# A short convolution by Strassen-Winograd products: partial sums formed in the accumulators, weight sums kept in DRAM after the first pass

## The reference, cut to what matters

```python
def _short_conv_mixer(xn, prev, w_in, conv_w, w_out):
    proj = xn @ w_in                       # 1024 -> 4 x 1024
    b_gate, c_gate, h, z = jnp.split(proj, 4, axis=-1)
    u = c_gate * h
    ...
    y = jax.nn.silu(z) * b_gate * conv     # conv: 3 taps over u
    return y @ w_out, up[:, T:]
```

## Time and profile before

| | us |
|---|---|
| median of 3 runs (lowest, highest) | 2836.79 (2834.07, 2838.17) |
| the profiled execution: its time | 2833.93 |
| its span, first to last instruction | 2832.2 |
| first matmul of the first product | 21.4 |
| last matmul of the phase's last product | 808.1 |
| PE busy over the whole span | 2690.6 |

### The profile page before, as it was taken

One profiled execution on the slowest core, in us unless ns is written; L12 is line 12 of the kernel. 1 busy time (PEld: TensorE's weight loads), 2 busy tenths in 40 slices (PEclk: granted clock), 3 DMA queues, 4 the chain that ended last, 5 costly groups with the idle time before them and its releaser, 6 DMA issues. The chain is left out here.

```text
span 2832.2 us, 44315 instructions
## 1 busy us (share of the span) xinstructions
PE 2690.6 (95%) x15048; PEld 2407.0 (85%) x15048; DVE 1998.5 (71%) x2590; ACT 1606.5 (57%) x3224; POOL 1435.6 (51%) x1251
## 2 busy tenths in 40 slices
PE   5997999799899999999989999999999999989998
PEld 5997999799888888889978988888888888877886
DVE  6777766877754460102248999999999999998775
ACT  5564454444333441111147888888888888875543
POOL 5767655776540021003346777777786768652110
PEclk8998999899999999999999999999999999999999
DMA  3332232133244443434578777767676866757873
GB/s 107 118 99 69 85 110 83 51 113 94 71 146 133 131 147 136 178 114 154 164 218 251 216 230 228 207 216 232 196 242 204 244 208 196 234 180 214 245 227 108
DMA packets 371536, 467.40 MB, mean 165 GB/s; under 512 B 53346, under 2 KB 312546, under 8 KB 365316
## 3 DMA queue, kind: packets, MB, share of 16 engines
q1 hardware_dynamic: 364612, 440.69, 51.4%
q0 software_dynamic: 6720, 24.13, 2.6%
HBM read 340.95 MB, written 123.81 MB: 164 GB/s over the span
## 5 line engine op out<-in xcount | busy, mean ns | idle before, releaser
L2318 POOL TENSOR_TENSOR a_a<-a_a,a_prod 128x512 f32<-128x512 f32 (+3 forms) x640 | 662.0, 1052 | 274.1 <-DVE a_prod L2269 196.9
L474 PE MATMUL c_pc<-c_xh,c_wh 128*128 128x384 f32 (+1 forms) x1344 | 453.3, 337 | 58.3 <-DVE c_sums L706 32.8
L2269 DVE TENSOR_TENSOR_SCAN a_prod<-a_keep,a_prod,a_restart 128x513 f32<-128x513 f32 x384 | 478.4, 1270 | 7.6 <-ACT a_keep L2213 7.0
L476 PE MATMUL c_pc<-c_xh,c_wl 128*128 128x384 f32 (+1 forms) x1344 | 449.2, 334 | 0.0
L475 PE MATMUL c_pc<-c_xl,c_wh 128*128 128x384 f32 (+1 forms) x1344 | 449.2, 334 | 0.0
L2212 ACT ACTIVATE a_a<-a_pz 128x512 f32<-128x512 f32 (+3 forms) x640 | 357.4, 559 | 70.2 <-PE a_pz L2139 48.5
L2279 DVE TENSOR_TENSOR a_atl<-a_pt,a_ath 128x512 fp32r<-128x512 f32 (+3 forms) x640 | 363.4, 600 | 31.9 <-ACT a_ath L2222 28.9
L2222 ACT ACTIVATE a_ath<-a_pt 128x512 fp32r<-128x512 f32 (+3 forms) x640 | 332.9, 559 | 56.9 <-PE a_po L2153 33.3
L2213 ACT ACTIVATE a_keep<-a_pz 128x512 f32<-128x512 f32 (+3 forms) x640 | 361.2, 565 | 0.0
L474 PEld LDWEIGHTS c_pc<-c_xh,c_wh 128*128 128x128 f32 x1344 | 261.5, 195 | 63.9 <-DVE c_sums L706 35.9
L2162 PEld LDWEIGHTS a_pt<-ident_r,a_bits 128*128 128x128 f32 x2176 | 231.0, 141 | 52.1 <-DVE a_atl L2279 8.4
(11 more groups left out here) (252 smaller groups left out, 5999.6 us busy)
## 6 DMA issues: line engine op xcount, KB each, us to landing
a_x<-x_d SPq DMA_DIRECT2D x84, 896.0 KB, 7.0
c_raw<-in_a_w_in SPq DMA_DIRECT2D x96, 512.0 KB, 4.1
a_x<-x_d SPq DMA_DIRECT2D x56, 832.0 KB, 5.6
a_kh<-kh_t SPq DMA_DIRECT2D x32, 512.0 KB, 7.1
a_kl<-kl_t SPq DMA_DIRECT2D x32, 512.0 KB, 9.1
x<-f_xn POOLq DMA_DIRECT2D x17, 512.0 KB, 5.2
g_y_in<-sz_t SPq DMA_DIRECT2D x17, 512.0 KB, 8.3
g_x<-x SPq DMA_DIRECT2D x17, 512.0 KB, 4.5
```

The costliest lines, as they stand in the source:

```text
L474: pe.matmul(o, room.wh[i][:, k, :], x_h, start=fresh and k == 0, stop=False, skip_group_check=True)
L476: mm = pe.matmul(o, room.wl[i][:, k, :], x_h, start=False, stop=k == NH - 1, skip_group_check=True)
L2269: dve.tensor_tensor_scan(prod[:, s, 0:w + 1][:, ::-1], keep[:, n % KS, 0:w + 1][:, ::-1], restart[:, 0:1].broadcast_to([P, w + 1]), prod[: ...
L2318: pool.tensor_tensor(part, part, prod[:, n % PS, after:after + w], ALU.mult).then_inc(weighted, 1)
```

## The change

**Passes** are (0, 384), (768, 384), (1536, 320), so six tiles are staged first and eleven later. **Accumulators:** S2_T2 is no longer the first product of bank C: ScalarE copies P1 from bank A into bank C (`move_p1`, PSUM to PSUM) and S2_T2, S3_T3 and A22_T4 add to it, so `v` and c21's sum with P1 are not formed. ScalarE copies S1_T1 (`read_p5`) and u2 (`read_u2`) to SBUF. Two small groups of matmuls at the start write bank C of both sets once. **Combining:** c21 is multiplied straight from PSUM by VectorE into `u` or `t`; GpSimd keeps `set_late_u`, two `gate` and `finish_late` for each pair. `sums` has a tile for each strip of a pair. **Weights:** GpSimd forms S1 to S4 in pass 0 alone, SP stores them to a DRAM tensor (`store_sum`, 256 KB each) and loads them in the passes after (`load_sum`); the raw A21 is then not loaded. `summed` is one semaphore for each sum. **Differences** are all VectorE's (`difference`), S1's and S3's one and two strips before the pass ends. **Tiles:** VectorE scales the first three; A11_B11 and A12_B21 of strip 0 need these alone. `turn` stands between A12_B21 and S4_B22, and ScalarE's `scale` behind `high(n, A22_T4)`. The three taps are loaded from GpSimd's queue.

```diff
-PASSES = [(0, 320), (640, 384), (1408, 384)]
+PASSES = [(0, 384), (768, 384), (1536, 320)]
...
         def _(sp):
...
+            for n in range(NSTRIP):
+                if n + 1 in norm_of:
+                    load_tile(norm_of[n + 1])
+                store_sum(n + 1, 2)
+                load_sum(n + 1, 2)
+                load_sum(n + 2, 0)
+                if n + 2 < NSTRIP:
+                    free_raw(n, 1)
                     load_raw(n + 2, 1)
                 if n >= 2 and n % 2 == 0:
                     store(n - 1)
+                load_sum(n + 2, 1)
                 if n + 3 < NSTRIP:
+                    free_raw(n + 1, 0)
                     load_raw(n + 3, 0)
+                load_sum(n + 2, 3)
+                for k in (0, 1, 3):
+                    store_sum(n + 2, k)
...
         def _(pe):
...
+            for n in range(1, NSTRIP):
                 product(n, A11_B11)
                 product(n, S1_T1)
+                product(n - 1, A22_T4)
                 product(n, S2_T2)
                 product(n, A12_B21)
+                if n - 1 in norm_of:
+                    turn(norm_of[n - 1])
                 product(n, S4_B22)
                 product(n, S3_T3)
...
         def _(act):
...
             for n in range(NSTRIP):
+                if n:
+                    move_p1(n)
                 high(n + 1, A11_B11)
+                if n and n % 2 == 0:
                     open_gate(n - 1)
+                if n % 2 == 0:
                     prefix(n)
+                if n:
+                    read_p5(n)
                 high(n + 1, S1_T1)
                 high(n, A22_T4)
+                if n - 1 in norm_of:
+                    scale(norm_of[n - 1])
+                if n % 2:
                     keep_and_tap(n)
+                if n:
+                    read_u2(n)
                 high(n + 1, S2_T2)
+                read_c11(n)
                 high(n + 1, A12_B21)
+                if n in norm_of:
+                    sums_of(norm_of[n])
                 high(n + 1, S4_B22)
                 high(n + 1, S3_T3)
...
         def _(dve):
...
             for n in range(NSTRIP):
+                p, turning = n // PER_PASS, n % PER_PASS == PER_PASS - 1 and n != LAST
+                if n and not first_of_pass(n):
                     c22(n - 1)
+                low(n, S3_T3)
                 low(n + 1, A11_B11)
+                if turning:
+                    difference(p + 1, S2_T2)
+                if n - 1 in norm_of:
+                    inverse(norm_of[n - 1])
                 low(n + 1, S1_T1)
                 if n:
                     c21(n - 1)
+                if first_of_pass(n):
+                    difference(p, A22_T4)
                 low(n, A22_T4)
                 if n % 2:
                     taps(n)
+                if p < NPASS - 1 and n % PER_PASS in (PER_PASS - 3, PER_PASS - 2):
+                    difference(p + 1, S1_T1 if n % PER_PASS == PER_PASS - 3 else S3_T3)
+                low(n + 1, S2_T2)
+                if turning:
+                    c22(n)
                 low(n + 1, A12_B21)
+                c12(n)
+                low(n + 1, S4_B22)
                 if n - 1 in norm_of:
+                    stage(norm_of[n - 1])
...
         def _(pool):
...
+            for k in (0, 1, 3, 2):
+                sum_weights(0, k)
+            for k in (0, 1, 3):
+                sum_weights(1, k)
             for n in range(NSTRIP + 1):
+                if n % 2:
+                    set_late_u(n - 1)
+                elif n:
                     gate(n - 1, 1)
+                    finish_late(n - 1)
+                sum_weights(n + 1, 2)
+                if n % 2:
+                    gate(n, 0)
+                for k in (0, 1, 3):
+                    sum_weights(n + 2, k)
```

More of the change, by code:

```diff
@@ L227 @@
 NPROD = 7
+SUMS = (S1_T1, S2_T2, S3_T3, S4_B22)
+EARLY_TILES = 3
 BANK_A, BANK_B, BANK_C = range(3)
@@ L265, in __init__ @@
         self.taps = put("c_taps", [P, KT, CW], F32, offset=room_at + 12288)
-        self.s = [put(f"c_s{i}", [P, NH, P], F32, offset=border.at + part * i) for i in range(4)]
+        self.s = [put(f"c_s{i}", [P, NH, P], F32, offset=border.at + part * i) for i in range(len(SUMS))]
         self.put, self.at = put, room_at + 28768
@@ L451, in product @@
                 p = STRIPS[n][0]
-                w, fresh = width(n), i in (A11_B11, S1_T1, S2_T2)
+                w, fresh = width(n), i in (A11_B11, S1_T1)
                 b = {A11_B11: BANK_A, A12_B21: BANK_A, S1_T1: BANK_B, S4_B22: BANK_B}.get(i, BANK_C)
@@ L611, in _ @@
             act.wait_ge(warm, 1)
-            for t in range(FIRST_TILES):
+            for t in range(EARLY_TILES + 1):
                 sums_of(t)
-                if t:
-                    scale(t - 1)
-                if t == 3:
-                    high_w(0, A11_B11)
-                elif t == 4:
-                    high_x(0, A11_B11)
-            scale(FIRST_TILES - 1)
-            high_w(0, S1_T1)
-            high_x(0, S1_T1)
-            for i in (S2_T2, A12_B21, S4_B22, S3_T3):
-                high(0, i)
@@ L625, in _ @@
[L625 to L630 removed]
+            scale(EARLY_TILES)
+            sums_of(EARLY_TILES + 1)
+            high(0, A11_B11)
+            scale(EARLY_TILES + 1)
+            high(0, A12_B21)
+            sums_of(EARLY_TILES + 2)
@@ L631, in _ @@
+            scale(EARLY_TILES + 2)
+            move_p1(0)
+            high(0, S1_T1)
+            high(0, S4_B22)
+            read_p5(0)
+            high(0, S2_T2)
+            high(0, S3_T3)
+            read_u2(0)
+            for n in range(NSTRIP):
+                if n:
+                    move_p1(n)
                 high(n + 1, A11_B11)
-                if m == 0 and n:
+                if n and n % 2 == 0:
                     open_gate(n - 1)
-                if m == 0:
+                if n % 2 == 0:
@@ L648, in _ @@
                 high(n + 1, A12_B21)
+                if n in norm_of:
+                    sums_of(norm_of[n])
                 high(n + 1, S4_B22)
                 high(n + 1, S3_T3)
-                if n in norm_of:
-                    sums_of(norm_of[n])
-                if n - 1 in norm_of:
-                    scale(norm_of[n - 1])
                 if n == LAST:
                     act.wait_ge(border.y_loaded, 16)
-                    for i in (S1_T1, S2_T2, S3_T3, S4_B22):
+                    for i in SUMS:
@@ L687, in stage, with difference @@
                                       gain[:, half].unsqueeze(2).broadcast_to([P, NH, P]), ALU.mult).then_inc(staged, 1)
+            def difference(p, i):
+                first, second, out, needs = {
+                    S1_T1: (room.quarter(p, 0, 1), room.quarter(p, 0, 0), room.operand(p, S1_T1), None),
+                    S3_T3: (room.quarter(p, 1, 1), room.quarter(p, 0, 1), room.quarter(p, 0, 1), S1_T1),
+                    S2_T2: (room.quarter(p, 1, 1), room.operand(p, S1_T1), room.quarter(p, 0, 0), S1_T1),
+                    A22_T4: (room.quarter(p, 1, 0), room.quarter(p, 0, 0), room.quarter(p, 1, 0), S2_T2)}[i]
+                order = (S1_T1, S3_T3, S2_T2, A22_T4)
+                dve.wait_ge(staged, tiles_staged(p))
+                if needs is not None:
+                    dve.wait_ge(t_set[order.index(needs)], p + 1)
+                if i == S2_T2:
+                    dve.wait_ge(x_lo[A11_B11], p + 1)
+                elif i == A22_T4:
+                    dve.wait_ge(x_lo[A12_B21], p + 1)
+                elif i == S1_T1:
+                    wait_past(dve, x_lo[S1_T1], p)
+                dve.tensor_tensor(out, first, second, ALU.subtract).then_inc(t_set[order.index(i)], 1)
             def low_x(p, i):
@@ L702, in low @@
                     low_x(STRIPS[n][0], i)
-            def add(out, n, b, other, read):
-                w = width(n)
-                dve.tensor_tensor(out, bank(n, b, w), other, ALU.add).then_inc(read, 1)
             def c22(n):
@@ L809, in _, with sum_weights @@
         def _(pool):
-            def sums(n):
+            def sum_weights(n, k):
+                if n >= PER_PASS:
+                    return
                 raw = room.raw[n % 2]
                 a11, a12, a21, a22 = raw[:, 0, 0:NH, :], raw[:, 0, NH:KT, :], raw[:, 1, 0:NH, :], raw[:, 1, NH:KT, :]
-                s1, s2, s3, s4 = (s[:, :, :] for s in room.s)
+                s = [tile[:, :, :] for tile in room.s]
+                first, second, op = ((a21, a22, ALU.add), (s[0], a11, ALU.subtract), (a11, a21, ALU.subtract),
+                                     (a12, s[1], ALU.subtract))[k]
@@ L2929, in build @@
     x1 = scratch("x1", [T, D])
+    sums_d = scratch("sums_d", [PER_PASS, len(SUMS), P, NH * P])
     x_d = scratch("x_d", [NGX, P, KT, 2, PW])
```

378 lines of the change are left out of this document (180 added, 198 removed).

## The result

| us | before | after |
|---|---|---|
| median (lowest, highest), 4 runs each on one chip | 2835.43 (2834.04, 2838.17) | 2759.28 (2757.80, 2760.17) |
| the profiled execution: its time, its span | 2833.93, 2832.2 | 2760.17, 2758.5 |
| first matmul of strip 0, of strip 1 | 21.4, 54.7 | 22.9, 56.6 |
| last matmul of the phase's last product | 808.1 | 729.8 |

The ratio is 0.973 (95% interval 0.9713 to 0.9747): 76 us faster, where 2758 was forecast. The phase is 78.3 us shorter by the profiles and the span 73.7. The code behind the phase is the same; over the fourteen profiles of this study it took 2023 to 2030 us, so the 4.6 between the two is no effect of the change.

A forecast was written before the change was run, and what follows sets the result against it. PE was taken as the bound, with 121 us above its pace in the phase. Gains of 30.1 + 29.6 + 14.5 + 3.0 + 1.0 = 78.2 us off 2833.9 gave 2755.7, forecast as 2758, range 2742 to 2786.

The forecast's parts named there:

- The turns: Token-tile transposes in passes 0 and 1: twelve PE waits of 1.92 us, slow clock and one turn go, 30.1 us won.
- The changes of pass: Strips around both pass changes: without GpSimd's weight sums stretching VectorE's subtractions, 29.6 us won, bounds 18 to 34.
- the uncontended walk: Step through strips 15 and 16 with VectorE at its undisturbed times: about 4.4 us lost at a change of pass.
- the contended 9.7: The same walk through strips 15 and 16 with VectorE contended: 9.7 us lost at a change of pass.
- The 7 and 6 that were to stay: Loss still expected after the change: 7 us at the first change of pass, 6 at the narrower second.
- The last pass: From 570 to 808.6 us: waits on c_sums behind GpSimd's late u go, 14.5 us won, bounds 8 to 15.5.
- The start: Up to strip 1: overhead falls from 44.1 to 41.1 us, 3.0 won, bounds 0 to 7; VectorE carries the chain.
- The steady state: Ordinary strips: ScalarE's added copies and the changed VectorE and GpSimd work were all to be hidden.
- the transfers: Loads and stores of weights and sums: DMA share about 0.6, each sum with some 13 us between issue and use.
- 7 us to spare: Pass 0 loop from raw load through three sums to u: sums end 2 to 3 us into the next strip, u due at 7.
- The rival that was to make it slower than before: Sum loads and stores on one queue hold each other up in all passes: 2878 at 5 us a pair; chance 0.04.
- The end: End of the phase: GpSimd's last `finish` falls out ahead of the last store, 1 us won.

The follow-up runs named there:

- u ahead: Kernel before, with GpSimd's second half of u put behind the first of the next strip's four weight sums instead of behind all four: 2871.37 us, ratio 1.0124.
- the third sum late: Kernel before, with GpSimd forming the next strip's sum S3 at the end of its strip, after the gates or second half of u: 2824.65 us, ratio 0.9967.
- the next weights late: Kernel before, with the roundings of the next phase's first five weight slabs all in the last strip, not one a strip from 39: 2831.86 us, ratio 0.9984.
- three copies a strip: Changed kernel, with three unread 512 KB DRAM-to-DRAM weight copies each strip ahead of the second raw load on SP's queue: 2820.3 us, ratio 0.9943.

## Why the prediction was right, step by step

**The turns: right, 30.1 forecast.** No wait of PE on `c_norm` is left from strip 2 on, and a turn costs 0.72, the own time that was put at 0.7. Won are 29.7, with 0.8 lost in strip 1. The slow clock that was counted in went with the idle time: the granted clock is 1.00 in 330 to 530 where it was 0.97. But the term is a place in the ledger, not the worth of the edit. Alone the edit brings 10 us (2833.29 to 2823.05), because in narrow strips `c_sums` takes the place of `c_norm`. The sum was right since the whole change takes that second wait away too, in pass 0 by the width and in the last pass by the new scheme; the prediction had no step for it, and that it came out is in part luck.

**The changes of pass: right, 29.6 forecast, 30.9 measured.** The releaser is the one named, `read_u2` behind the high part of T4, and the first change keeps 6.2, between the 4.4 of the uncontended walk and the contended 9.7. The 7 and 6 that were to stay are 6.2 and 6.0. One low granted stretch of 3.4 us remains in each (windows 280 to 330 and 530 to 575 at 0.97 and 0.96). VectorE's two stretched operations in strip 16 end 0.5 and 1.6 us after GpSimd's. The prediction read the earlier trace rows as an end together with GpSimd's instruction; it too is 0.5 later (247.6 after 247.1), most of the operation's own 0.68. The Trainium skill (SBUF — State Buffer, Who interferes with whom) has one engine held there for the whole of the other's instruction; the trace agrees, 2.56 us for an operation that takes 1.75. By its rule with GpSimd idle the change would have kept 4.4; GpSimd was not idle: the stretch beside its `gate` and `finish`, 1.6 us, is in size nearly the 1.8 between.

**The last pass: right in size (14.5 and 15.3) and in the chain, without the cause ahead of it.** "The chain there: ScalarE's keep_and_tap waits 4.54 us for GpSimd's u, since `set_u` stands behind the sums of the next strip" is what the rows of strips 43 and 44 show, with taps, c22 and PE behind it. But u behind the sums is in every pair; what makes it late in strips 40 to 45 are the next phase's roundings ahead of c22, which the prediction did not name: without them 13 us of stall go. Of the 15.7, moving u ahead wins 2.8 and moving S3 behind u 6.8. The changed kernel keeps the roundings in the same strips and loses 0.4 there, since GpSimd forms no sums; with them (sums in every pass) 5.4 us come back in just these strips. The edits to the kernel before were run one by one, none of them together.

**The start: 3.0 forecast, nothing won.** The 44.1 of overhead stay 44.1. This lies on the lower bound of 0 to 7, and may lie below it. Three of the kernels made from the one before (u ahead, the third sum late, the next weights late) have its code up to strip 1 but for the place of a sum, and reach strip 1 at 52.8, 53.3 and 52.9, where its own profile has 54.7; four with the changed kernel's start reach it at 56.4 to 57.7, beside its 56.6. 1.9 us of the difference are more work (12.5 for 10.6), so against the usual 52.9 the start has become some 2 us slower; the profile of before had a long one. The kernel before with the turn alone agrees, at 52.6. Three parts of the walk were too short. VectorE's reciprocal stands for tile 3, whose square waits for its transfer, and `stage` 1 and 2 stand behind it; the low parts and differences run beside GpSimd's sums and are stretched (the one at 20.07 ends at 22.88, 1.6 us after GpSimd's sum of 19.77 to 21.28); and PE at half clock makes what waits for its products late. Timeline of the changed kernel, the rows for each:

```profile
15.31 0.16 DVE L739 RECIPROCAL c_rstd<-c_std 128x1 f32<-128x1 f32 x1 [2.60 <-ACT c_std L568]
...
20.07 2.81 DVE L778 TENSOR_TENSOR c_xl<-c_stage,c_xh 128x1536 fp32r<-128x1536 f32 x1
...
44.29 2.54 POOL L924 TENSOR_TENSOR c_s<-c_raw,c_s 128x512 f32<-128x512 f32 x1 [0.22 <-issue]
...
45.61 2.84 DVE L773 TENSOR_TENSOR c_stage<-c_stage 128x1536 f32<-128x1536 f32 x1
...
40.80 0.49 ACT L611 ACTIVATE c_p<-c_pc 128x384 f32<-128x384 f32 x1 [4.54 <-PE c_pc L507]
```

The first was tested (the start in another order) and is worth 3.2 us at the first product and about 1 behind strip 2. The other two are read from rows, not tested. VectorE's own scaling was no part of it: 0.75 us where 1.1 was taken.

**The steady state, the transfers, the end.** All of what was called hidden is hidden: no wait in 330 to 530, and 0.4 us in 60 to 280. The third copy of ScalarE, into PSUM, takes 0.47. The DMA share is 0.53 and 0.49, forecast about 0.6, and the stores of the sums land in 2.2 us at the median (60 to 280). "I find 7 us to spare" in the loop of pass 0 was wrong, though it cost nothing: in strip 9, which starts at 176.94, the third sum ends 4.4 us in where 2 to 3 were told, and u at 182.8, 1.2 us ahead of `keep_and_tap`. GpSimd and ScalarE in the timeline of the changed kernel:

```profile
180.06 1.29 POOL L924 TENSOR_TENSOR c_s<-c_raw,c_s 128x512 f32<-128x512 f32 x1 [0.22 <-issue]
181.31 1.46 POOL L939 TENSOR_TENSOR c_u<-c_sums,c_cg 128x384 f32<-128x384 f32 x1
...
183.97 0.20 ACT L656 ACTIVATE c_carry<-c_u 128x2 f32<-128x2 f32 x1
```
Loads 1 us slower to land, with the copy's issue ahead of them, cost 5 us. The rival that was to make it slower than before would have needed the loss in all passes; three copies a strip give 2820, with 2.0 us of it in the steady strips of passes 1 and 2. The end (1.0 forecast) is 0.3: 3.5 us of wait into the next phase, where it was 3.8.

**The sum.** That 2758 lies 1.3 us from 2759.28 is closer than the terms are. The start and the end gave 3.7 us less than forecast, the changes and the last pass 2.1 more, the narrow pace and the changed widths 2.4 that no term held, and the unchanged code behind the phase varies by more than that between profiles.

## What to carry to other kernels

A ledger of where the bound engine stands above its pace gives the total of a rewrite well, but not the worth of each edit: a second wait may lie just under the first, as it did in the narrow pass 0, where some 11 us of waits for the turns went and 4 us more than these came back. A wait row names who came last and not why it was late; follow the late engine back, in order of time, to the first work that is out of its usual place, and check that a wait ends before the stall that it is to explain. Read an experiment in the strips that it was aimed at: moving u ahead won 3 us there and lost 37 in the two passes before. Work taken off an engine that is not the bound pays only in the stretches where it holds others up: 83 us of 200 off GpSimd gave nothing in a steady pass, and some 17 in all at the passes' changes and in four strips near the end.

## What the runs showed of the hardware

Rows of the changed kernel: a ScalarE copy from PSUM to PSUM, and VectorE's scaling of one SBUF operand by a column.

```profile
268.20 0.47 ACT L606 ACTIVATE c_pc<-c_pc 128x384 f32<-128x384 f32 x1 [1.45 <-PE c_pc L507]
```

```profile
6.41 0.75 DVE L743 TENSOR_SCALAR c_norm<-c_x_first,c_rstd 128x1024 f32<-128x1024 f32 x1
```

The copy inside PSUM costs nearly what one to SBUF does (means of 0.475 and, in two places, 0.484 and 0.489 for 128x384). The scaling handles 1024 columns in 0.75 us, where the subtraction of two SBUF operands takes 0.68 for 512 and 1.75 for 1536, so an estimated 1.2 for 1024: with one tensor read it takes about 0.6 of the time. The Trainium skill (VectorE: DVE Perf Modes, Mode 2×_2P) says that an operation with one tensor in SBUF uses both read ports on it, float32 too; the trace agrees in the direction. And a queue that carries 1.5 MB more a strip delays the landing of a 512 KB load by 2.7 us at the median (4.6 to 7.3), not by the time of the copies ahead of it (5.9 each to landing): transfers of one queue overlap in good part.

VectorE and GpSimd, each with two operands in SBUF, hold each other for whole instructions. A pair of the changed kernel's start:

```profile
42.79 1.28 POOL L924 TENSOR_TENSOR c_s<-c_s,c_raw 128x512 f32<-128x512 f32 x1 [7.91 <-DVE c_wl L785]
...
43.21 2.47 DVE L778 TENSOR_TENSOR c_xl<-c_stage,c_xh 128x1536 fp32r<-128x1536 f32 x1 [0.68 <-ACT c_xh L585]
```

In four places of the changed kernel a VectorE operation of 1.75 us starts while GpSimd's is under way and ends 1.60 to 1.62 us after GpSimd's end (22.88 after 21.28, 45.68 after 44.07, 48.45 after 46.83, 292.20 after 290.58). The other way round, GpSimd's sums that start at 21.44 and 44.29 end 1.14 and 1.15 us after VectorE's, where such a sum takes 1.29 alone. In these rows the later one does most of its work after the other is done, so two that overlap cost nearly the sum of both.
